# The rests of every second normed tile move from VectorE to GpSimd

## The reference

```python
def modulate(h, shift, scale):
    return h * (1.0 + scale) + shift

def swiglu(u, wg, wu, wd):
    return (jax.nn.silu(u @ wg) * (u @ wu)) @ wd

u = modulate(rmsnorm(h, norm_ffn1[l]), mod[:, :, 0], mod[:, :, 1])
h = h + 0.5 * (1.0 + mod[:, :, 2]) * swiglu(u, ffn1_wg[l], ffn1_wu[l], ffn1_wd[l])
```

## Time and profile before

| | |
|---|---|
| median of 3 runs | 2103.79 us (2102.07 to 2104.55) |
| profiled execution, its own time | 2109.59 us |
| its span, first to last instruction | 2107.8 us |
| mean granted TensorE clock | 0.979 |
| TensorE / VectorE / ScalarE / GpSimd busy | 95% / 69% / 48% / 4% of the span |
| instructions on GpSimd | 77 |

### The profile page before, as it was taken

One profiled execution on the slowest core, in us unless ns is written; L12 is line 12 of the kernel. 1 busy time (PEld: TensorE's weight loads), 2 busy tenths in 40 slices (PEclk: granted clock), 3 DMA queues, 4 the chain that ended last, 5 costly groups with the idle time before them and its releaser, 6 DMA issues.

```text
span 2107.8 us, 37384 instructions
## 1 busy us (share of the span) xinstructions
PE 2008.9 (95%) x15792; PEld 1955.3 (93%) x15792; DVE 1450.6 (69%) x2203; ACT 1016.4 (48%) x1565; POOL 88.2 (4%) x77
## 2 busy tenths in 40 slices
PE   4999999999999999999999989998999899999999
PEld 3999999989999999999899979897999898989998
DVE  6777787777677667867767667656767777546554
ACT  3444655454455445663544455443544453525443
POOL 0000002100000000022000000000000000000000
PEclk8999999999999999999999989999999999999999
DMA  8877565457776776645587745455777564344542
GB/s 338 296 262 272 207 239 188 175 210 282 275 262 235 271 274 218 253 172 187 192 318 269 268 166 199 173 190 180 270 270 261 202 201 171 132 148 149 191 181 101
DMA packets 83849, 466.37 MB, mean 221 GB/s; under 512 B 9440, under 2 KB 9568, under 8 KB 44512
## 3 DMA queue, kind: packets, MB, share of 16 engines
q1 hardware_dynamic: 46496, 326.00, 42.5%
q10 hardware_dynamic: 37184, 137.97, 18.1%
HBM read 462.88 MB, written 1.05 MB: 220 GB/s over the span
## 4 chain that ended last, share of the span: by engine, by line
PE 69%; DVE 6%; ACT 3%; issue 1%; DMA 1%; POOL 0%; DVEq 0%; ACTq 0%; SPq 0%
PE bank L631 68%; DVE low L1512 2%; ACT high L1089 1%; DMA ring<-stream 1%; DVE ada_ring L1494 1%; PE bank L878 1%; DVE tmp L1550 0%; ACT tmp L1336 0%; DVE region L1914 0%; DVE region L1869 0%; ACT rs L1109 0%; ACT rs L1112 0%; ACT merged L1432 0%; ACT u_high L1126 0%; DVE u_low L1555 0%
## 5 line engine op out<-in xcount | busy, mean ns | idle before, releaser
L631 PE MATMUL bank<-u_high,high 128*128 128x256 f32 x3232 | 923.2, 286 | 39.9 <-DVE u_low L1555 37.0
L631 PE MATMUL bank<-u_high,low 128*128 128x256 f32 x3232 | 911.8, 282 | 0.0
L631 PE MATMUL bank<-u_low,high 128*128 128x256 f32 x3232 | 911.1, 282 | 0.0
L1512 DVE TENSOR_TENSOR low<-ring,high 128x1024 fp32r<-128x1024 f32 (+1 forms) x600 | 722.2, 1231 | 159.5 <-ACT high L1089 145.6
L1089 ACT ACTIVATE high<-ring 128x1024 fp32r<-128x1024 f32 (+1 forms) x600 | 597.6, 1042 | 136.4 <-PE bank L631 107.8
L631 PEld LDWEIGHTS bank<-u_high,high 128*128 128x128 f32 x3232 | 613.7, 190 | 47.8 <-DVE u_low L1555 37.7
L631 PEld LDWEIGHTS bank<-u_low,high 128*128 128x128 f32 x3232 | 614.1, 190 | 2.7 <-issue 1.4
L631 PEld LDWEIGHTS bank<-u_high,low 128*128 128x128 f32 x3232 | 613.5, 190 | 0.4
L631 PE MATMUL bank<-xa,high 128*128 128x256 f32 x2368 | 423.6, 280 | 0.9 <-DVE low L1512 0.9
L631 PEld LDWEIGHTS bank<-xa,high 128*128 128x128 f32 x2368 | 361.8, 188 | 3.2 <-DVE low L1512 1.5
L631 PE MATMUL bank<-xa,low 128*128 128x256 f32 x1184 | 330.9, 279 | 0.0
(11 more groups left out here) (178 smaller groups left out, 1615.2 us busy)
## 6 DMA issues: line engine op xcount, KB each, us to landing
ring<-stream SPq DMA_DIRECT2D x302, 1024.0 KB, 5.6
ada_ring<-ada ACTq DMA_DIRECT2D x242, 512.0 KB, 4.5
region<-ada ACTq DMA_DIRECT2D x7, 1024.0 KB, 22.4
ring<-stream SPq DMA_DIRECT2D x4, 640.0 KB, 4.0
region<-na_bias ACTq DMA_DIRECT2D x2, 1024.0 KB, 5.4
ring<-stream SPq DMA_DIRECT2D x4, 512.0 KB, 4.8
cst<-const ACTq DMA_DIRECT2D x1, 1600.0 KB, 20.9
cond<-cond SPq DMA_DIRECT2D x2, 512.0 KB, 7.5
```

Of the source, the lines that this page charges most:

```text
L631: return pe.e.matmul(out, lhs, rhs, start=start, stop=stop, skip_group_check=True)
L1512: dve.e.tensor_tensor(lo, src, hi.bitcast(F32), ALU.subtract).then_inc(*dve.done(("low", n)))
```

## The change

In `norm(s)` of VectorE's program, the rest is made for tiles 0, 2, 4 and 6 only. GpSimd's program gets a `norm(s)` of its own for tiles 1, 3, 5 and 7: it waits for `u_high`, adds the shift to the scaled tile in place (a column of 128 values, one per partition), waits for that instruction's completion, and subtracts `u_high` into `u_low`. It stands ahead of the mixer's work in each of the ten stages. The sum has the same two steps as the one instruction of before.

```diff
@@ dve_program, norm(s)
             if d > 0 and s[0] not in ("fin", "out"):
                 e = d - 1
+                if e % 2:
+                    continue
                 dve.wait_ge(("u_high", s, e))
...
@@ pool_program
+    def norm(s):
+
+        _, _, shift = norm_of(m, s)
+        for e in range(1, KT, 2):
+            pool.wait_ge(("u_high", s, e))
+            x = m.normed[:, e % 4, :]
+            pool.e.tensor_scalar(x, x, m.mod(shift)[:, e:e + 1], None, ALU.add).then_inc(*pool.done(("shifted", s, e)))
+            pool.wait_ge(("shifted", s, e))
+            pool.e.tensor_tensor(m.ul[:, e, :], x, m.uh[:, e, :].bitcast(F32), ALU.subtract) \
+                .then_inc(*pool.done(("u", s, e)))
+
...
     for s in STAGES:
+        if s[0] not in ("fin", "out"):
+            norm(s)
         if s[0] == "m1":
             mixer1(s)
```

## The result

| | before | after |
|---|---|---|
| median of the runs, us | 2102.93 (4 runs, 2099.07 to 2104.55) | 2133.65 (4 runs, 2124.69 to 2136.85) |
| profiled execution, its own time, us | 2109.59 | 2136.85 |
| its span, us | 2107.8 | 2135.1 |
| mean granted TensorE clock | 0.979 | 0.973 |

The change makes the kernel slower: the ratio is 1.0134 [1.0110, 1.0158], 30.7 us between the medians, 27.3 us between the two spans.

The account below looks back on a forecast made before the run. TensorE's work plus its waits was taken to bound the kernel. Five FFN stages 13.0, first stage 1.6, m1 3.8, m2 13.6, less 2.0, make +30.0 us on 2103.8: forecast 2133.8, range 2117 to 2148.

Parts of the forecast that it names:

- Point 1: Norm: VectorE loses 40 rests of 0.40 us, 16 us of work; alone this saves nothing.
- Point 2: Norm, GpSimd: 40 additions at 0.52 us (ends 0.31, 0.74), 40 subtractions at 0.70; odd rest takes 1.3.
- The rival of a quick addition: GpSimd's addition in the norm as quick as a memset, 0.31 us: +20, 2124 us; chance 0.18.
- The rival of a slow addition: GpSimd's addition in the norm as long as a product of twice the columns: 30 more, 2164 us; chance 0.10.
- Point 3: Norm: GpSimd and VectorE take turns at SBUF, whole instructions, no loss between; +1.9 us a stage, +1.1 in the first.
- that rival: Hand-overs between VectorE and GpSimd cost 0.14 us, seven in each of ten stages: 10 us more, 2144; chance 0.08.
- my schedule: Norm's order of turns for VectorE and GpSimd; tile 7 ready 10.06 us after the first scaling, last tile today 6.97.
- the signs that I named: GpSimd busy about 50 us more, scalings' mean near 0.7 instead of 0.50, last rest about 10 us after first scaling.
- 6 us widening of the range: Clock staying low for longer after the new gaps: 6 us on the range's high side.
- Point 4: After norm: next grain's rest collides with last subtraction; 0.7 us in five later FFN stages, 0.5 first, 0 in m1.
- Point 5: m2: window addition behind the norm delays grain rests, +4.9 us each time; second m2's first scaling no longer blocked, -2.0.
- The rival on the other side: Norm: instructions this short may not exclude each other; +1 us, 2105; chance 0.06.

Follow-up runs that it names:

- fourth: Changed kernel with window addition back ahead of the norm, GpSimd's shift addition left out: 2104.76 us, ratio 1.0009 to the kernel before.
- sixth runs: Changed kernel with window addition back ahead of the norm, ScalarE adds the shift, GpSimd only subtracts: 2107.62 us, ratio 1.0012 to the kernel before.
- seventh run: Changed kernel with window addition back ahead of the norm, GpSimd makes only tile 7's rest: 2112.33 us, ratio 1.0032 to the kernel before.

## Why the prediction was right, and where it was not

**The whole.** Forecast 2133.8, measured 2133.65, inside the range. The direction and both parts (norms and window addition) were right. That the numbers meet to 0.2 us is luck: the four groups of stages in the table were off by 18 to 33%, some up and some down, the addition's length by 75%, and the four runs of the changed kernel alone spread over 12 us. The working has two slips as well. The first pair's end at 10.9 less 9.1 is 1.8 and not 1.9, which takes 0.9 us from the sum; and the range as described (+20 less 4.4, +41 and 6) is 2119 to 2151, not 2117 to 2148. The measured time lies inside either.

**Point 1, VectorE's 16 us save nothing:** the fourth and sixth runs agree, in which it has them and the time is the same. No run takes them from VectorE without loading GpSimd, so a gain that the turns ate up is not excluded.

**Point 2, the addition at 0.52:** wrong, 0.912 at least. The step that failed is the interpolation between a memset and a two-tensor instruction. A memset reads nothing, and the upper bound rested on the thought that one tensor in costs less than two; the row of after says the opposite (0.912 against 0.728). The rival of a quick addition is out by the same row; the Trainium skill, "GPSIMD Engine Reference", section "Engine selection", which calls one-input operations roughly line-rate, does not agree with it, as far as one column count can tell (a rate and a fixed start are not parted here). The rival of a slow addition (1.27) is nearer, though not because of the column: that is 0.07 of it.

**Point 3, whole-instruction turns:** right for the subtraction, wrong for the addition. The two scalings at 445.77 start beside a subtraction that ends at 446.44 (445.71 + 0.73); 446.44 and their own 0.88 are 447.32, and the row ends at 447.33. Nothing is left over for a hand-over. Nor is there in the other direction: in the seventh run VectorE's grain rest ends at 445.33 (444.10 + 1.23) and GpSimd's subtraction at 445.91, 0.58 us later, less than its own 0.73. So that rival is out too, and the 115 ns that the Trainium skill gives in "SBUF — State Buffer", section "A bandwidth-pool intuition that's wrong (but worth ruling out)", are not seen here. The addition, however, holds VectorE far less than it is long: the scaling at 444.76 takes 0.69 beside an addition of 0.92, that is 0.2 more than alone, and the rests at 443.26 and 445.38 keep their 0.48 and 0.47 while additions run. The one that was held started 0.05 us behind the addition's start, the other two 1.00 and 0.67 us behind it; whether only the start of an addition holds VectorE was not tried. So an addition of 0.92 that holds little stood in for one of 0.52 that holds all. Measured from the first scaling, the odd rests are there at 3.98, 5.70, 7.64 and 9.94, where my schedule had 3.5, 5.5, 8.3 and 10.06. Of the signs that I named, the scalings' mean became 0.58 us, not 0.7.

**Which tile bounds.** I had tile 7 set the end of the first pair, and put no clock cost on the holes. The trace has another path. TensorE stands at tile 1 for 0.9 to 1.6 us in all ten stages, and the low level of the clock ends later behind that. At tile 5 it never waits, and at tile 7 only in ("f1", 1) and ("f2", 1), for 0.3 and 0.1 us. The price is nearly the same by either path, since tile 7, ready at 9.94, allows a first pair of no less than 9.94 + 0.14 + 0.71 - 1.69 = 9.1 us, and the eight stages other than m2 lie between 9.1 and 9.9. The longer low level was in the text only as a 6 us widening of the range; it is in fact what makes the difference between 9.1 and 9.9. The two stages that wait for tile 7 have the high clock back after 5.3 and 6.0 us and take 9.12; in the other six the first pair grows with that time, from 9.21 us with the clock back after 6.4 to 9.91 after 8.0. The experiments on tiles 1, 3, 5 and 7 show both limits apart.

**Point 4, the grain rest and the last subtraction:** the tie came about as described (1.31 instead of 0.73 in the changed kernel, 1.69 in the seventh run), VectorE had the turn, and it was free in the change because tile 7 was not yet needed. My 0.7 a stage was paid, but by the clock.

**Point 5, the window addition:** right in place and mechanism. The 4.9 us of waiting came as 4.2 and 3.8 more of standing still; the term lacked what a hole of 4 us does to the clock behind it, 2.7 and 1.5 more in the second pair. The gain at the second m2, 2.0, came as 1.9. At the first m2, where I had put nothing, the 1.2 ahead of the norm is the clock's, as shown above.

**The rival on the other side,** that instructions this short do not exclude each other, half holds for the additions and still does not save the change: the addition's own length is enough to bring tile 1 too late.

## What to carry to other kernels

When work moves to an engine that is idle, time the first result that the busy engine needs, not the last: a first result that came 1.5 us late was followed by a later return of TensorE's high clock, and then hid how late everything behind it was. Move an instruction in series only where its length on the new engine has a row; where it has none, its neighbours bound it poorly, so widen the bound beyond both. In a queue that runs in order, look at what stands behind the moved work: here it was one 4.5 us instruction that shares its access with the grain rests, and cutting it into pieces away from them was worth more (0.2%, half of it seen in the trace) than the relief, which bought nothing that could be measured. A stage's length in one trace also holds where the clock happened to be low; look at the granted clock before a difference is put down to the edit.

## What was unexpected of the hardware

- GpSimd's addition of a column to 128x256 float32 takes 0.912 us at least (0.92 with VectorE idle) and one with a constant 0.841, longer than a subtraction of two tensors of that size at 0.728.
- Exclusion between GpSimd and VectorE depends on the instruction: a two-tensor subtraction holds VectorE until it ends, the one-tensor addition for about 0.2 us or not at all. The other way, the first addition of a norm, started 0.06 us after two scalings of VectorE, took 1.52 us, that is until 0.7 us after their end. What in the instruction makes the difference was not settled; the column is a part of it, since with a constant the same addition took 1.14.
- A hole of 1.5 us soon after TensorE resumes moved the return of the high clock from 4.9 to 7.7 us after the first matmul in stage ("f2", 0), more than the hole itself, but in ("f1", 1), with a hole as long, only from 4.9 to 5.3.
- ScalarE's wait for the sum of squares ahead of a norm is 1.25 us at the high clock and up to 2.52 where the low level reaches into it (granted clock 0.62).
- Beside a piece of the window addition a 128x2 operation of VectorE (L1819), otherwise 0.17 us, took 0.64 to 0.66: the wait for a turn has nothing to do with the size of what waits.
